# Weight loads laid out as one 16 KB piece per partition, in a layer with routed experts

## What is computed

```python
sh1, sc1, gt1, sh2, sc2, gt2 = ada_mod(cond, lp['w_ada'], lp['b_ada'])
h = rms_norm(x, lp['norm1_g']) * (1.0 + sc1) + sh1
q, k, v, hy = split_projection(h @ lp['w_in'])
att = attend(q, k, v)
hyo = hyena_mixer(hy, lp)
merged = jnp.concatenate([rms_norm(att, lp['gnorm_att']), rms_norm(hyo, lp['gnorm_hyena'])], axis=-1)
x = x + gt1 * (merged @ lp['w_out'])
h2 = rms_norm(x, lp['norm2_g']) * (1.0 + sc2) + sh2
x = x + gt2 * hier_moe(h2, lp)
```

## Time and profile before

| | us |
|---|---|
| median of 3 runs | 835.08 (833.68 to 836.03) |
| the profiled execution, its own time | 832.79 |
| its span | 831.1 |
| outside the span | 1.7 |

### The profile page before, as it was taken

One profiled execution on the slowest core, in us unless ns is written; L12 is line 12 of the kernel. 1 busy time (PEld: TensorE's weight loads), 2 busy tenths in 40 slices (PEclk: granted clock), 3 DMA queues, 4 the chain that ended last, 5 costly groups with the idle time before them and its releaser, 6 DMA issues. The chain is left out here.

```text
span 831.1 us, 10457 instructions
## 1 busy us (share of the span) xinstructions
PE 719.1 (87%) x3772; PEld 544.2 (65%) x3772; DVE 531.9 (64%) x799; ACT 407.1 (49%) x602; POOL 167.1 (20%) x168
## 2 busy tenths in 40 slices
PE   2898999899999989999985389999999989999800
PEld 1248998849898755555544368877777777778600
DVE  5345526367512057565435669999988999999648
ACT  1454533411223144555322357777777677777433
POOL 2000000000022047542210302333333333331000
PEclk9999999999999989999987589999999999999955
DMA  9993115211398191000008983999999999999163
GB/s 325 407 400 114 58 45 203 101 43 73 128 179 320 65 394 44 1 26 2 26 26 274 396 303 106 372 377 365 352 362 362 355 357 347 360 363 361 55 269 128
DMA packets 67196, 183.75 MB, mean 221 GB/s; under 512 B 4592, under 2 KB 4624, under 8 KB 63824
## 3 DMA queue, kind: packets, MB, share of 16 engines
q1 hardware_dynamic: 58080, 161.39, 52.2%
q0 software_dynamic: 7312, 19.61, 6.8%
q10 hardware_dynamic: 1760, 2.17, 0.8%
HBM read 175.26 MB, written 14.19 MB: 228 GB/s over the span
## 5 line engine op out<-in xcount | busy, mean ns | idle before, releaser
L1407 DVE TENSOR_TENSOR WL<-slot,WH 128x1024 fp32r<-128x1024 f32 x192 | 222.0, 1218 | 1.3 <-ACT WH L970 1.0
L970 ACT CAST WH<-slot 128x1024 fp32r<-128x1024 f32 x192 | 187.1, 1052 | 25.5 <-DMA slot<-in_w_up 16.0
L1606 PE MATMUL bank<-WH,xgTh 128*128 128x512 f32 x256 | 103.7, 405 | 17.8 <-DVE WL L1407 16.4
L1606 PE MATMUL bank<-hTh,WP 128*128 128x384 f32 (+1 forms) x320 | 99.6, 311 | 2.2 <-DVE hT L1123 2.2
L1606 PE MATMUL bank<-WL,xgTh 128*128 128x512 f32 x256 | 101.0, 394 | 0.0
L1606 PE MATMUL bank<-WH,xgTl 128*128 128x512 f32 x256 | 100.9, 394 | 0.0
L1606 PE MATMUL bank<-hTl,WP 128*128 128x384 f32 (+1 forms) x320 | 99.4, 311 | 0.0
L1606 PE MATMUL bank<-hTh,WL 128*128 128x384 f32 (+1 forms) x320 | 99.4, 311 | 0.0
L1510 PE MATMUL bank<-slot,big 128*128 128x512 f32 (+1 forms) x224 | 91.7, 559 | 1.6 <-issue 1.6
L705 POOL DMA_INDIRECT y_scratch<-big x16 | 67.1, 4196 | 108.5 <-DVE big L1440 108.5
L1519 PE MATMUL bank<-ident,big 128*128 128x128 f32 x424 | 62.2, 287 | 14.0 <-DMA big<-h_scratch,big 8.2
(11 more groups left out here) (226 smaller groups left out, 1081.4 us busy)
## 6 DMA issues: line engine op xcount, KB each, us to landing
slot<-in_w_gate SPq DMA_DIRECT2D x16, 2048.0 KB, 14.0
slot<-in_w_up SPq DMA_DIRECT2D x16, 2048.0 KB
slot<-in_w_down SPq DMA_DIRECT2D x16, 2048.0 KB, 9.2
slot<-in_w_ada SPq DMA_DIRECT2D x12, 2048.0 KB, 13.1
slot<-in_w_in SPq DMA_DIRECT2D x6, 2048.0 KB, 17.4
big<-in_x SPq DMA_DIRECT2D x2, 2560.0 KB, 20.4
big<-y_scratch SPq DMA_DIRECT2D x5, 1024.0 KB, 8.9
big<-m_scratch POOLq DMA_DIRECT2D x8, 512.0 KB, 9.1
```

The costliest lines, as they stand in the source:

```text
L970: act.copy(WH[:, high_half(w, s), r, :], quarter(s, w, r)).then_inc(high_ok[w], 1)
L1407: dve.tensor_tensor(WL[ESLOT[3 * s + w]][:, r, :], quarter(s, w, r), WH[:, high_half(w, s), r, :].bitcast(F32), ALU.subtract).then_inc(low ...
L1606: ins = pe.matmul(out, l[u], r[v], start=first and i == 0, stop=last and i == 2)
```

## The change

Before the launch the host rearranges `w_ada`, `w_in`, `w_out`, `w_gate`, `w_up` and `w_down` so that, for each load of 2 MB, the 16 KB of a partition lie together in DRAM. The loads then copy one piece of 16 KB per partition. What lands in the slot is the same as before; order, slots, waits and bytes stay.

```diff
@@ chunk_src
             if c[0] == "ada":
-                return a["w_ada"][c[2] * 2 * P:(c[2] + 1) * 2 * P, c[1] * AW:(c[1] + 1) * AW].rearrange("(k p) n -> p k n", p=P)
-            w = {"win": a["w_in"], "wout": a["w_out"]}[c[0]]
-            return w[:, c[1] * 512:(c[1] + 1) * 512].rearrange("(k p) n -> p k n", p=P)
-
-        def chunk_view(i):
-            return slot[IN_SLOT[i]].rearrange("p (k n) -> p k n", n=AW if CHUNKS[i][0] == "ada" else 512)
+                return a["w_ada"][c[1], c[2]]
+            return {"win": a["w_in"], "wout": a["w_out"]}[c[0]][c[1]]
@@ load_chunk
-                src = chunk_src(CHUNKS[i])
-                if len(src.shape) == 2:
-                    src = src.rearrange("p (k n) -> p k n", n=512)
-                sp.dma_start(chunk_view(i), src).then_inc(chunk_in[IN_SLOT[i]], 16)
+                sp.dma_start(slot[IN_SLOT[i]], chunk_src(CHUNKS[i])).then_inc(chunk_in[IN_SLOT[i]], 16)
@@ load_expert
-                    n = 512 if j < 2 else 1024
-                    src = src.rearrange("a (k p) n -> p (a k) n", p=P)
-                    sp.dma_start(slot[ESLOT[3 * s + j]].rearrange("p (k n) -> p k n", n=n), src)\
+                    sp.dma_start(slot[ESLOT[3 * s + j]], src.rearrange("a p n -> p (a n)"))\
                       .then_inc(ew_in[3 * s + j], 16)
@@ kernel (on the host)
+    def rows(w, cuts, parts):
+
+        n = w.shape[-1] // cuts
+        v = w.reshape(*w.shape[:-2], parts, -1, P, cuts, n)
+        return np.moveaxis(v, (-2, -5, -3, -4), (-5, -4, -3, -2)).reshape(*w.shape[:-2], cuts, parts, P, -1)
...
-        "w_ada": g["w_ada"][0], "b_ada": quads(g["b_ada"][0].reshape(ADA_GROUPS, 4, 512)), "w_in": g["w_in"][0],
-        "w_out": g["w_out"][0], "w_gate": g["w_gate"][0], "w_up": g["w_up"][0], "w_down": g["w_down"][0],
+        "w_ada": rows(g["w_ada"][0], ADA_GROUPS, ADA_PARTS), "b_ada": quads(g["b_ada"][0].reshape(ADA_GROUPS, 4, 512)), "w_in": rows(g["w_in"][0], 6, 1)[:, 0],
+        "w_out": rows(g["w_out"][0], 2, 1)[:, 0], "w_gate": rows(g["w_gate"][0], 1, 1)[:, 0, 0], "w_up": rows(g["w_up"][0], 1, 1)[:, 0, 0], "w_down": rows(g["w_down"][0], 1, 1)[:, 0, 0],
```

## The result

| | before | after |
|---|---|---|
| median, same chip | 834.50 us (833.68 to 836.03, 4 runs) | 860.03 us (853.50 to 862.94, 4 runs) |
| ratio of the runs | | 1.0298 (95% interval 1.0257 to 1.0340) |
| the profiled execution, its span | 832.79, 831.1 | 853.50, 851.8 |
| its mean granted clock | 0.936 | 0.931 |

The change made the kernel 3.0% slower. The forecast of 855 and its range of 826 to 872 hold.

The account below looks back on a forecast made before the run. The expert stage was taken as paced by how soon a small scatter gets through queues full of weight loads. Terms -0.6 + 3.5 + 4.2 + 13.2 = +20.3 gave 853 us profiled, 855 as median; own range 845 to 866, 8 in 10 826 to 872.

Parts of the forecast that it names:

- the ring: Expert steps: keep_rows, result copy, scatter, its landing, then keep_rows again; the scatter's passage through queues of weight loads sets the pace.
- Turns packet by packet: Shared DMA engines: two queues alternate by packet, so each full scatter row waits 615 ns for a 16 KB piece, before 87.
- Rival 2: Weight loads: 16 KB pieces served in turns of 4 KB, 0.6 us a step over 14 steps, 843 us; chance 0.07.
- Start: Ahead of the ada piece TensorE waits for at 49.58 us: one w_in load gets shorter, -0.6 us.
- Middle: From 60 to 440 us: no change, 0, because TensorE is full and covers loads that land sooner.
- Entry: Entry to the experts: TensorE's wait for the first gather, beside gate, up and down loads, grows by 3.5 us.
- First scatter: At about 523 us: its loads, issued only 10 us before, do not run dry, so +4.2 us.
- Later steps: Twelve further expert steps: +1.1 us each, 13.2 in all, capped because the loads run dry and everything lands 19.9 us after issue.
- The delay before the first packet: Between a scatter's last descriptor (618.2) and its first packet (621.4): 3.2 us, taken as unchanged.
- Rival 3: Expert steps faster: that 3.2 us backlog before the scatter's first packet shrinks; floor 820 us, half of it 827; chance 0.16.
- Rival 1: Expert steps: longer TensorE gaps lower its clock too, adding 10 to 20 us, 865 to 875 us; chance 0.13.
- Rival 4: Whole kernel: nothing, as less work and longer turns cancel or the scatter's engines are free by then; 835 us; chance 0.08.

Follow-up runs that it names:

- e7: Kernel before (old layout) with four scatter-index columns in place of two, so keep_rows waits for a scatter two steps older, and expert steps written out: 828.66 us, ratio 0.9944.
- e10: Control: the changed kernel with its expert steps written out instead of looped and nothing else, two index columns kept: 859.08 us, ratio 1.0292.
- e2: Kernel before with only w_ada, w_in and w_out in 16 KB pieces, expert weights left in rows of 2 and 4 KB: 832.70 us, ratio 0.9993.
- e4: The changed kernel's 16 KB pieces for gate and down, but up left in rows of 2 KB: 839.48 us, ratio 1.0090 against the kernel before.
- e8: Changed kernel with four scatter-index columns in place of two, so keep_rows waits for a scatter two steps older, and expert steps written out: 822.92 us, ratio 0.9862.

## Why the prediction was right, point by point

- **What bounds the kernel** (the ring, not bandwidth): shown by e7 to e10. Loads that land sooner made the kernel slower while the ring stood, and faster once it was cut.
- **Turns packet by packet, at 16 KB as well:** 64 against 66. Rival 2 (turns of 4 KB) falls with it, and the dose from 4 to 16 KB agrees. The unit of 9 to 17 descriptors that the Trainium skill gives for a packet ("DMA: Bandwidth & Descriptors", Queues, rings and completion order) shows no more at 16 KB than it did before.
- **Start, -0.6:** -0.38. The ada piece's product starts at 49.20 where it started at 49.58. Mis-sized by 0.2.
- **Middle, 0:** the window at 226 to 290 is the same; e2 confirms it, 0.9993.
- **Entry, +3.5:** the wait grew by 3.2 (8.25 to 11.46), and the first expert transposes came 2.64 us later (472.96 to 475.60), the start's gain included.
- **First scatter, +4.2:** +3.7 (19.53 to 23.25), made of 4.1 more for the packets and 0.4 less before the first of them. The eight full packets per row engine are an inference still; the size fits, and no row names the engines.
- **Later steps, +1.1 each by the ceiling:** +1.2 (19.54 to 20.74). That it is a ceiling is shown by the first scatter's step against the later ones, 23.25 and 20.74, and by the landings 19.5 and 20.0 us after the loads' issue, where the forecast had 19.9. The mean hides an alternation of 19.8 to 21.8 us.
- **The sum as a whole, 853 against 853.5:** closer than its terms. The first scatter was set 0.5 us too high and the start and entry 0.2. Twelve further steps were put at 13.2 us; eleven came to 13.3 already, and the twelfth, in which `keep_rows` had no wait before the change, to 3.2 more. The end, put at 0, came out 2.2 us shorter. That these cancel is luck. The spread of the terms given for 845 to 866 (entry 0 to 4.2, 0.6 to 1.7 a step) adds up to 846 to 863 only; nothing in the sum gives the upper 3 us.
- **The delay before the first packet, left as it is:** right to 0.3 us. The forecast read 3.2 us; with narrower windows it is 3.4 in that scatter. In the twelve scatters of the steps it is 3.4 to 3.7 us before and 2.9 to 3.6 in the changed kernel, 3.5 and 3.2 on average; in e4 it is 3.3 to 4.3. Rival 3 needed it to shrink by more than the turns grew; it shrank by 0.3 us.
- **Rival 1, the clock:** it does fall, but what that costs in the steps is not shown. Before, the granted clock was 1.00 from 510 to 700 us. In the changed kernel three stretches of the expert steps fall to the lower level; two of them, in the columns of the windows:

```profile
536.80:540.20 3.40, 3.40 (x9) 2.68 (x9) 3.40 (x5) 1.28 (x2) 0.00 (x0) 0.50 1.00 426
577.80:581.20 3.40, 2.86 (x7) 2.29 (x8) 3.40 (x4) 1.40 (x2) 0.05 (x1) 0.50 0.97 413
```

  They stand behind waits for the scatter; 5.24 us at 533.56 and 3.80 at 575.36 are the two longest, while the third stretch, at 745, stands behind one of 2.85. The executions of 862.8 and 862.9 us had a mean clock of 0.921 and 0.919, but those of 853.5 and 857.3 us both had 0.931. The profile of e10, an execution of 860.42 us with the same layout, has 0.94 in the window of the steps where the changed kernel's has 0.98, that is some 29 us at the lower level against 10:

```profile
520.00:760.00 240.00, 214.05 (x996) 172.98 (x995) 199.82 (x236) 158.40 (x191) 72.98 (x23) 0.94 0.85 337
```

  Its rows of `keep_rows` show how little of its 6.8 us (span 858.6 against 851.8) lies there:

```profile
512.84 0.15 DVE L1379 COPY big<-big 128x1 int32<-128x1 int32 x1
...
785.65 0.15 DVE L1379 COPY big<-big 128x1 int32<-128x1 int32 x1 [1.27 <-DMA y_scratch<-big]
...
802.34 0.15 DVE L1379 COPY big<-big 128x1 int32<-128x1 int32 x1
```

  Against 510.31, 781.76 and 798.44 of the changed kernel e10 is 2.5 us behind at the first row and 3.9 at the other two. So 2.5 us are there before the first scatter, 1.4 come in the thirteen steps with all the falls, and 2.9 behind the last row, where from 802.34 to 818.57 the clock is 0.89 (in the changed kernel 1.00, 798.44 to 812.31). Before, the median lay 1.7 us above the profiled execution, now 6.5: some 5 us of the loss are spread between executions of the same kernel. The clock may be a part of that spread, at the entry and at the end rather than in the steps; no kernel was made that changes the clock alone. The 865 to 875 that this rival gave were not reached.
- **Rival 4 and the rule of the Trainium skill on bandwidth** ("DMA: Bandwidth & Descriptors", Bandwidth: HBM's limit of about 358 GB/s per core binds; the section gives that figure for two cores that stream from one HBM domain, and here one core runs): the "nothing" did not come. The window at 536.8 above has 426 GB/s, and over 220 us e8 moved 383, e7 367; by that rule e8 would have gained nothing over e7.

## What to carry to other kernels

Before making a load's pieces larger, list the small transfers that share its DMA engines and ask which of them a pipeline waits for: each of their packets will stand behind one piece of the load, so the piece's size is their price. Larger pieces pay (here 10% of the loads' engine time, 6 us) once those small transfers have a step of slack or the loads are held back for the moment in which one matters; without that, the same change cost 26 us. And a DMA share near 1 does not show that bandwidth paces a kernel: here only the cut ring made it true.

## What was not expected of the hardware

- A scatter's first packet waits 2.9 to 4.3 us after its last descriptor with loads in the other queue (averages of twelve: 3.5 before, 3.2 at 16 KB, 3.7 in e4), and this does not grow with the size of the packets. In three scatters of e10 (issued at 544.62, 670.34 and 756.02), whose loads had left SP 9 to 10 us ahead and ended soon, it is 1.3 to 2.2 us. With nothing in the other queue it is 0.6 us: in the kernel before a scatter's descriptors are ready at 782.24, and its packets start behind 782.8. So the loads hold it back, but by what is open.
- From 8 to 16 KB the loss per step stays level (20.83 and 20.74 us), because at 16 KB the loads run dry; for a transfer whose neighbour never runs dry it grows on, 20.88 and 23.25 us.
- In e8, with every wait for the scatter gone, TensorE held the full clock through 220 us, 1.00, at 217.84 us busy.
